# Transposing attention probabilities in 32x32 blocks on VectorE with SBUF-to-SBUF transfers, and a new order of the first loads

## The chip, the cores and the metric

The kernel runs on one core of a Trainium2 chip. The metric is the time of one execution on the device in microseconds (us), and lower is better.

## What is computed

One encoder layer runs over two token sequences, a prompt of 512 tokens and a sample of 1024, laid side by side as 1536 tokens of width 1024, all in float32:

```python
h = RMSNorm(x)
a_val, a_glu, z_a, q, k, v, z_b, g_logits = split(h @ w_in)         # 9 x 1024 columns
y_a = (silu(LayerNorm(conv31(a_val * sigmoid(a_glu)))) * silu(z_a)) @ w_pw_a
# 16 heads; every query sees an 8 x 16 window of the (rows, 64) token grid, with a learned bias
p = softmax(where(valid, q @ k.T / 8 + bias, -1e30))
y_b = ((p @ v) * silu(z_b)) @ w_o_b
x + (sigmoid(g_a) * y_a + sigmoid(g_b) * y_b) @ w_out               # then a final RMSNorm
```

## The kernel before, in words

**Matrix products.** Every float32 operand is kept as a high and a low part, and a product of 128x128 weights with 512 tokens is three matmuls (low x high, high x low, high x high). A group is one 128-column tile of the weights times 512 tokens: 8 contraction steps, 24 matmuls into one of two PSUM banks (pg). Half a group, 12 matmuls, is called a slot, and slots are the clock by which all engines' instruction lists are written.

**Prologue.** SP loads the token tiles x and the first weight pieces (L409 to L424). ACT's queue issues six loads of small parameters and the load of norm_g (L655 to L658). VectorE multiplies each token tile by its reciprocal norm and norm_g (`normalise`, L1011), TensorE transposes it (`h_t`), ACT writes the high part and VectorE the low part (`h_hi`, `h_lo`). Then v is projected, and the tiles of the first head pair.

**Units.** There are 8 units, one for each pair of heads. Unit 0 and unit 7 are written out and have 36 slots each, units 1 to 6 are a hardware loop body of 48 slots. In each unit TensorE projects the next tiles while attention of the head pair is woven in between. Attention has 12 blocks of 128 queries in each unit. A block sees 256 keys (blocks 0 to 3) or 384 keys (blocks 4 to 11), for each of two heads. Blocks are taken in pairs. `pair_at` puts a pair at slot 1 and then every `2 * spacing(i)` slots: 4 slots in units 0 and 7, 6 slots in the loop. The work of a pair goes like this:

- At its slot TensorE first does `values` of the pair before (L1464, which waits for pt_ok), and then `scores` (L1435) into four PSUM banks pS.
- VectorE adds bias and mask and takes the minimum (`scores`, L1143), ACT takes the exponential with its sum (L841), VectorE takes the reciprocal (L1151) and multiplies (L1153). The first block of the pair is done in the pair's slot, the second one slot later, behind a convolution tap (`tap`, L1069) and the evacuation of a group.
- `transposed_at` sets the slots at which TensorE transposes the probabilities 128x128 at a time into PSUM (`transposes`, L1455, 512 of them), and ACT copies them back to SBUF (`probs_t`, L844).
- `take_o` (L1155) multiplies the result in PSUM bank pO by the gate.

**SP's queue.** SP runs down one list. In a unit it loads weight pieces (`piece`, L394), each behind a wait for the low part of the piece that held the buffer (w_lo), then the relative bias of the next unit (`load_rel`, 16 transfers) and its v (`load_v`, 16 transfers, behind pv_done). Behind unit 7 it waits for pv_done of all blocks and loads seven tiles of 768 KB of the gated attention (tb_d, L497), which ACT and VectorE split in `refill_tb` (L765), called at slots 33 and 35 of unit 7 and behind it.

GpSimd builds the bias tiles (L580) as VectorE frees them.

Of the kernel before, what the change touches and what calls it, by code (L numbers as in the profile page):

```python
# [24 lines left out]
F32 = mybir.dt.float32  # L25
# [79 lines left out]
def spacing(i):  # L105

    return 2 if isinstance(i, int) else 3
# [40 lines left out]
def build(nc, x_prompt, x_sample, norm_g, w_in, b_gate, dw_w, dw_b, ln_g, ln_b, w_pw_a, rpb,  # L148
          w_o_b, w_out, final_g, masks, y_prompt, y_sample):
    with ExitStack() as ctx:  # L150
# [26 lines left out]
        tt = take(4 * 384).rearrange("p (s n) -> p s n", s=4)  # L177
        pt = take(4 * 384).rearrange("p (s n) -> p s n", s=4)
# [75 lines left out]
        pT = ctx.enter_context(nc.psum_tensor("pT", [P, CH], F32))  # L254
        pO = ctx.enter_context(nc.psum_tensor("pO", [P, CH], F32))

        pH = [pT, pO, pS[2], pS[3]]
# [34 lines left out]
        tr_done, pt_ok, pv_done, o_out = (sem(n) for n in ("tr_done", "pt_ok", "pv_done", "o_out"))  # L292
# [82 lines left out]
        def transposed_at(i, slot, half):  # L375

            m = 4 * spacing(i)
            c, r = divmod(2 * slot + half - 2, m)
            t = r - (6 if spacing(i) == 3 else 4)
            if 0 <= t < 4 and 0 <= c < BLOCKS // 2:  # L380
                return 2 * c + t // 2, t % 2
            return None
# [10 lines left out]
        def _(sp):  # L393
# [16 lines left out]
            for s in range(4):  # L410
                piece_s(s, w_rows(w0, C_V * P, s))
                if s % 2:
                    load_x(1 + s // 2)
            for t in range(3, 8):
                load_x(t)
            for s in range(4, 6):
                piece_s(s, w_rows(w0, C_V * P + CH, s - 4))

            sp.wait_ge(w_lo, 4)
            sp.dma_start(msk32, masks).then_inc(mask_in, 16)  # L420
            for t in range(8, NT):
                load_x(t)
# [35 lines left out]

            def unit(i):
# [5 lines left out]
                for n, c in enumerate(ahead):  # L465
                    s = s_of(i) + n + 2
                    piece(s, w_tile(w0, i * P + c * P), 8 * i + (s - 1))
                    if n == len(ahead) - 3 and not last:
                        load_rel(i + 1, 18 * i + 18)
                    if n == len(ahead) - 2 and not last:  # L470
                        load_v(i + 1, BLOCKS * i + BLOCKS)
# [6 lines left out]
            def piece_y(s):  # L478
                if s < S_OUT:
                    piece_s(s, w_tile(w_o_b[0] if s < S_YA else w_pw_a[0], (s - S_YB) % KT * P))  # L480
                else:
                    piece_s(s, w_rows(w_out[0], CH * ((s - S_OUT) // 4), (s - S_OUT) % 4))

# [5 lines left out]

            piece_y(S_YB)  # L490
            piece_y(S_YB + 1)
# [55 lines left out]
        def _(pool):  # L547
# [21 lines left out]
            def unit(i):  # L569
                for kd in range(KINDS):  # L570
                    for h in range(2):
                        s, jk = kd // 3, kd % 3
                        nk = SEG_ROWS[s] * BAND
                        if kd == 0:
# [6 lines left out]
                            bt[:, 2 * (kd % 2) + h, 0:nk].rearrange("p (r c) -> p r c", c=BAND),  # L581
                            mask[:, KIND_OFF[kd]:KIND_OFF[kd] + nk].rearrange("p (r c) -> p r c", c=BAND),
                            e, ALU.subtract).then_inc(bias_ok, 1)
# [41 lines left out]
        def _(act):  # L625
# [29 lines left out]
            for r, n, src in ((0, TAPS, dw_w[0]), (I_DWB, 1, dw_b[0:1, :]), (I_LNG, 1, ln_g[0:1, :]),  # L655
                              (I_LNB, 1, ln_b[0:1, :]), (I_BGA, 1, b_gate[0:1, 0:D]), (I_BGB, 1, b_gate[0:1, D:2 * D])):
                act.dma_start(prow[r:r + n, :], src).then_inc(par_in, 16)
            act.dma_start(ngb, norm_g[0:1, :].to_broadcast([P, D])).then_inc(ng_in, 16)  # L658

# [8 lines left out]
            def h_hi(t):  # L668
                for hf in range(2):
                    act.wait_ge(ht_ps, 2 * t + hf + 1)  # L670
                    nc.scalar.activation(xs[:, 4 * hf:4 * hf + 4, 0, t * P:(t + 1) * P],
                                         pH[(2 * t + hf) % 4][:].rearrange("p (k n) -> p k n", k=4),
                                         ACT.Copy).then_inc(x_hi, 1)
# [15 lines left out]
            split_s(0)  # L689
            split_s(1)  # L690
            square(1)
            h_hi(0)
            split_s(2)
            split_s(3)
            for t in range(NT):
                if t + 2 < NT:
                    square(t + 2)
                if t + 1 < NT:
                    h_hi(t + 1)
                    take_v(t)  # L700
                if t == 4:
                    split_s(4)
# [68 lines left out]
            def unit(i):  # L771
# [64 lines left out]
                def probs(b, h):  # L836
# [3 lines left out]
                    t = tt[:, x, 0:keys_of(b)]  # L840
# [3 lines left out]
                def probs_t(b, h):  # L844
                    act.wait_ge(tr_done, blk(i, b, h))

                    after(act, pv_done, BLOCKS * i + max(b - 1, 0))
                    nk = keys_of(b)
                    nc.scalar.activation(pt[:, buf(b, h), 0:nk], pT[:, 0:nk], ACT.Copy).then_inc(pt_ok, 1)  # L849

                for slot in range(2 * NCH * len(tiles)):
# [9 lines left out]
                    for half in range(2):  # L861
                        bh = transposed_at(i, slot, half)
                        if bh is not None:
                            probs_t(*bh)
# [12 lines left out]
                    if slot == spacing(i) * BLOCKS + 2 and not last:  # L877
# [105 lines left out]
        def _(dve):  # L983
# [29 lines left out]
            def h_lo(t):  # L1013
                for hf in range(2):
                    dve.wait_ge(x_hi, 2 * t + hf + 1)
                    nc.vector.tensor_tensor(xs[:, 4 * hf:4 * hf + 4, 1, t * P:(t + 1) * P],
                                            pH[(2 * t + hf) % 4][:].rearrange("p (k n) -> p k n", k=4),
                                            xs[:, 4 * hf:4 * hf + 4, 0, t * P:(t + 1) * P].bitcast(F32),
                                            ALU.subtract).then_inc(x_lo, 1)

            mean_square_x(0)
            split_s(0)
            normalise(0)
            split_s(1)
            mean_square_x(1)
            h_lo(0)
            split_s(2)
            normalise(1)
            split_s(3)
            for t in range(1, NT):  # L1030
                if t + 1 < NT:
                    mean_square_x(t + 1)
                h_lo(t)
                if t + 1 < NT:
                    normalise(t + 1)
                if t == 5:
                    split_s(4)
                    dve.wait_ge(par_ps, 1)
                    nc.vector.tensor_copy(par[:].rearrange("p k n -> p (k n)"), pS[0][:, 0:KT * NPAR]).then_inc(par_ok, 1)
# [7 lines left out]
            for s in range(5, 10):  # L1047
                split_s(s)
# [81 lines left out]
            def unit(i):  # L1130
# [4 lines left out]
                def scores(b, h):  # L1135
# [4 lines left out]
                    after(dve, tr_done, 24 * i + max(blk(0, b - 2, h), 0))  # L1140
# [3 lines left out]
                        out=tt[:, x, 0:nk], in0=pS[x][:, 0:nk], in1=bt[:, 2 * (kind_of(b) % 2) + h, 0:nk], scale=1.0,  # L1144
                        scalar=3e38, op0=ALU.add, op1=ALU.min, accum_out=mn[:, x:x + 1]).then_inc(t_ok, 1)

                def probs(b, h):
                    x = buf(b, h)
                    t = tt[:, x, 0:keys_of(b)]
# [3 lines left out]
                    nc.vector.tensor_scalar(t, t, rinv[:, x:x + 1], None, ALU.mult).then_inc(p_ok, 1)  # L1153

                def take_o(s):  # L1155
# [6 lines left out]
                    o = pO[:].rearrange("p (j r c) -> p j r c", j=4, c=QB)  # L1162
# [22 lines left out]
                for slot in range(slots):  # L1185
# [5 lines left out]
                    if c is not None and c >= 2 and c % 2 == 0:  # L1191
                        take_o(c // 2 - 1)
                    if c is not None and c < BLOCKS // 2:
# [3 lines left out]
                        for h in range(2):  # L1197
                            probs(2 * c, h)
                    c = late_pair_at(i, slot)
# [150 lines left out]
        def _(pe):  # L1350
            PASSES = ((1, 0), (0, 1), (0, 0))

            def half_group(b, s, n, hf, ready=None, midway=None):
# [227 lines left out]
```

## Time and profile before

| | |
|---|---|
| median of 3 runs | 1835.28 us (1830.8 to 1837.01) |
| the profiled execution | 1836.65 us, its span 1834.8 us |
| TensorE matmul busy | 1795.8 us, 98% of the span |
| VectorE, ScalarE, GpSimd busy | 1093.2, 549.8, 210.0 us |
| mean granted TensorE clock | 0.994 |
| DMA on SP's queue | 111.44 MB, 20.3% of 16 engines' span |

The profile is of one execution. Busy time of an engine is the time in which one of its instructions ran. Matmuls are pipelined, so what one costs is read from the distance between starts, not from its own duration. SPq and ACTq are the instructions by which a queue issues transfers, and they are not counted as busy time.

### The profile page before, as it was taken

How to read it: one execution, taken by the hardware profiler on the slowest of the kernel's cores; microseconds unless marked ns; L12 is line 12 of the kernel's file. 1: busy time of each engine (PE TensorE's matmuls, PEld its weight loads, DVE VectorE, ACT ScalarE, POOL GpSimd, SP SyncE). 2: the span in 40 equal slices, each digit the busy share in tenths (PEclk: the TensorE clock that was granted, in tenths of full speed). 3: DMA queues.
4: the chain of work that ended last, by engine and by line, in shares of the span. 5: the costliest groups of instructions: out<-in, count | busy, mean ns of one | idle time of the engine just before them, and what ended most of it. 6: DMA issues, size and time to landing. Idle time of an engine off the chain costs nothing.

```text
span 1834.8 us, 25369 instructions
## 1 busy us (share of the span) xinstructions
PE 1795.8 (98%) x9164; PEld 1463.8 (80%) x9164; DVE 1093.2 (60%) x1573; ACT 549.8 (30%) x1117; POOL 210.0 (11%) x250
## 2 busy tenths in 40 slices
PE   6999999999999999999999999999999999999998
PEld 5888878888888888888888888888887777888786
DVE  3410695785587387558648837856874667535432
ACT  4411134233223323313322332332345233202122
POOL 0030011011011101101101110110110045000001
PEclk9999999999999999999999999999999999999999
DMA  7163101312211221231230223123116756543223
GB/s 272 53 116 92 41 30 53 92 58 87 75 42 64 78 73 52 81 88 47 86 87 30 69 70 87 53 81 87 35 58 240 253 156 200 167 137 104 92 81 126
DMA packets 163357, 174.03 MB, mean 95 GB/s; under 512 B 11238, under 2 KB 117750, under 8 KB 163098
## 3 DMA queue, kind: packets, MB, share of 16 engines
q1 hardware_dynamic: 136848, 111.44, 20.3%
q10 hardware_dynamic: 22506, 47.08, 6.8%
q0 software_dynamic: 3872, 13.75, 3.0%
q8 instruction: 84, 1.38, 0.3%
q14 instruction: 47, 0.39, 0.1%
HBM read 121.55 MB, written 50.68 MB: 94 GB/s over the span
## 4 chain that ended last, share of the span: by engine, by line
PE 89%; DVE 5%; DMA 3%; ACT 1%; issue 1%; SPq 0%; ACTq 0%; POOLq 0%; POOL 0%; DVEq 0%
PE pg L1361 65%; PE pg L1379 14%; PE pO L1476 3%; PE pT L1461 3%; PE pS L1451 3%; DVE work L1255 1%; DMA qk<-gb_d 1%; DVE work L1069 1%; DMA work<-tb_d 1%; DMA work<-in_norm_g 1%; DVE ws L987 1%; DVE xs L995 0%; ACT xs L763 0%; ACT ws L631 0%; DVE work L1261 0%
## 5 line engine op out<-in xcount | busy, mean ns | idle before, releaser
L1361 PE MATMUL pg<-xs,ws 128*128 128x512 f32 x5760 | 1384.1, 396 | 7.0 <-DVE work L1272 7.0
L1361 PEld LDWEIGHTS pg<-xs,ws 128*128 128x128 f32 x5760 | 1068.2, 189 | 233.8 <-issue 14.8
L1069 DVE SCALAR_TENSOR_TENSOR work<-work 128x1551 f32<-128x1551 f32 x240 | 449.4, 1873 | 4.1
L1379 PE MATMUL pg<-ws,xs 128*128 128x512 f32 x1008 | 239.8, 394 | 3.0 <-DVE ws L987 2.4
L1379 PEld LDWEIGHTS pg<-ws,xs 128*128 128x128 f32 x1008 | 189.8, 190 | 44.5 <-DVE ws L987 3.7
L987 DVE TENSOR_TENSOR ws<-raw,ws 128x1024 fp32r<-128x1024 f32 x90 | 109.9, 1222 | 137.3 <-ACT ws L631 137.2
L1143 DVE CUSTOM_DVE_ANT_0 work<-pS,work 128x384 f32<-128x384 f32 (+1 forms) x192 | 88.8, 511 | 166.1 <-PE pS L1451 165.7
L580 POOL TENSOR_TENSOR work<-work 128x384 f32<-128x384 bf16 (+1 forms) x72 | 63.1, 877 | 1052.3 <-DVE small L1143 1039.2
L841 ACT ACTIVATE work<-work,small 128x384 f32<-128x384 f32 (+1 forms) x192 | 109.2, 570 | 218.3 <-DVE small L1143 218.3
L849 ACT ACTIVATE work<-pT 128x384 f32<-128x384 f32 (+1 forms) x192 | 87.3, 454 | 170.3 <-PE pT L1461 170.2
L631 ACT ACTIVATE ws<-raw 128x1024 fp32r<-128x1024 f32 x90 | 94.6, 1053 | 110.3 <-PE pg L1361 83.3
L1153 DVE TENSOR_SCALAR work<-work,small 128x384 f32<-128x384 f32 (+1 forms) x192 | 97.5, 508 | 6.8
L1461 PEld LDWEIGHTS pT<-ident,work 128*128 128x128 f32 x512 | 67.7, 140 | 26.8 <-DVE work L1153 1.7
L1461 PE MATMUL pT<-ident,work 128*128 128x128 f32 x512 | 87.0, 272 | 1.3 <-DVE work L1153 1.3
L580 POOL TENSOR_TENSOR work<-work,ws 128x384 f32<-128x384 bf16 (+1 forms) x72 | 66.5, 924 | 55.2 <-DMA ws<-rel_d 55.2
L1476 PEld LDWEIGHTS pO<-work 128*64 128x64 f32 x1024 | 54.9, 137 | 17.0 <-issue 17.0
L1476 PE MATMUL pO<-work 128*64 128x128 f32 x1024 | 66.5, 277 | 0.0
L1095 DVE SCALAR_TENSOR_TENSOR work<-work 128x512 f32<-128x512 f32 x24 | 17.6, 731 | 75.4 <-ACT work L813 62.9
L1328 DVE TENSOR_TENSOR work<-pg,work 128x512 f32<-128x512 f32 x24 | 16.6, 692 | 75.3 <-PE pg L1379 75.2
L1276 DVE SCALAR_TENSOR_TENSOR work<-qk,pg 128x512 f32<-128x512 f32 x24 | 16.5, 687 | 73.2 <-PE pg L1361 73.2
L824 ACT ACTIVATE work<-pg,work 128x512 f32<-128x512 f32 x48 | 33.0, 687 | 74.1 <-PE pg L1361 74.0
L1163 DVE TENSOR_TENSOR work<-pO,work 128x512 f32<-128x512 f32 x24 | 16.6, 691 | 57.5 <-PE pO L1476 57.5
(100 smaller groups left out, 960.8 us busy)
## 6 DMA issues: line engine op xcount, KB each, us to landing
raw<-in_w_in SPq DMA_DIRECT2D x70, 512.0 KB, 3.8
work<-v_d SPq DMA_DIRECT2D x128, 96.0 KB, 3.0
v_d<-work ACTq DMA_DIRECT2D x24, 256.0 KB, 2.0
za_d<-work ACTq DMA_DIRECT2D x24, 256.0 KB, 2.0
ga_d<-work ACTq DMA_DIRECT2D x24, 256.0 KB, 2.0
gb_d<-work ACTq DMA_DIRECT2D x24, 256.0 KB, 2.0
work<-c_d POOLq DMA_DIRECT2D x8, 768.0 KB, 13.2
qk<-gb_d SPq DMA_DIRECT2D x24, 256.0 KB, 4.0
```

Of the source, the lines that this page charges most:

```text
L580: nc.gpsimd.tensor_tensor(bt[:, 2 * (kd % 2) + h, 0:nk].rearrange("p (r c) -> p r c", c=BAND), mask[:, KIND_OFF[kd]:KIND_OFF[kd] + nk].rea ...
L631: nc.scalar.activation(wt(s, 0), raw_of(s), ACT.Copy).then_inc(w_hi, 1)
L841: nc.scalar.activation(t, t, ACT.Exp, scale=-1.0, bias=mn[:, x:x + 1], accum_out=rsum[:, x:x + 1]).then_inc(p_exp, 1)
L849: nc.scalar.activation(pt[:, buf(b, h), 0:nk], pT[:, 0:nk], ACT.Copy).then_inc(pt_ok, 1)
L987: nc.vector.tensor_tensor(wt(s, 1), raw_of(s), wt(s, 0).bitcast(F32), ALU.subtract).then_inc(w_lo, 1)
L1069: nc.vector.scalar_tensor_tensor(cv[:, 0:CLEN], u[:, k:k + CLEN], cur[:, k:k + 1], cv[:, 0:CLEN], ALU.mult, ALU.add).then_inc(tap_ok, 1)
L1143: nc.vector.tensor_tensor_reduce(out=tt[:, x, 0:nk], in0=pS[x][:, 0:nk], in1=bt[:, 2 * (kind_of(b) % 2) + h, 0:nk], scale=1.0, scalar=3e38 ...
L1153: nc.vector.tensor_scalar(t, t, rinv[:, x:x + 1], None, ALU.mult).then_inc(p_ok, 1)
L1361: last = nc.tensor.matmul(pg[b][:], wt(s, wpart)[:, k * P:(k + 1) * P], xs[:, k, xpart, chunk(n)], start=(k == 0 and wpart == 1), stop=(k ...
L1379: last = nc.tensor.matmul(pg[b][:], xs[:, k, xpart, t * P:(t + 1) * P], wt(s0 + k // 2, wpart)[:, chunk(k % 2)], start=(k == 0 and xpart = ...
L1461: mm = nc.tensor.transpose(pT[:, c * P:(c + 1) * P], tt[:, buf(b, h), c * P:(c + 1) * P], ident[:])
L1476: mm = nc.tensor.matmul(pO[rows, j * P:(j + 1) * P], vb[:, SEG_RG[s] + c, j, rows], pt[:, buf(b, h), c * P:(c + 1) * P], start=(c == 0), s ...
```

## The change

The 128x128 transposes on TensorE and ACT's copies go. VectorE transposes each head's probabilities in place, as a grid of 32x32 blocks, right behind the multiplication. SP then moves the blocks between partition groups: for each block of queries 16 transfers (4 source groups of 32 partitions times 4 target groups), of 32 partitions x 2 heads x 256 or 384 bytes each. The keys are ordered by quadrant so that each quarter is contiguous; scores, bias, mask and values follow that order. A semaphore for each block parity (p_in) lets `values` start. pT's PSUM bank becomes a second bank of pO, and `take_o` comes behind scores and the first probabilities. A pair comes every 5 slots in units 0 and 7 and every 6 in the loop, as `pair_at` divides by `spacing(i)` now. SP's `move_probs` of a pair stands behind the weight piece of the same index. In the last unit the pieces S_YB and S_YB+1 move in between. In the prologue norm_g and the small parameters are loaded by SP, norm_g second; x tiles come later than the first weight pieces; `params` on TensorE comes behind the first 12 token groups, and `normalise(0)` ahead of the first split on VectorE.

```diff
 def spacing(i):
-    return 2 if isinstance(i, int) else 3
+    return 5 if isinstance(i, int) else 6
...
         def pair_at(i, slot):
-            c, r = divmod(slot - 1, 2 * spacing(i))
+            c, r = divmod(slot - 1, spacing(i))
...
             load_x(0)
-            for s in range(4):
+            sp.dma_start(ngb, norm_g[0:1, :].to_broadcast([P, D])).then_inc(ng_in, 16)
+            for s in range(2):
                 piece_s(s, w_rows(w0, C_V * P, s))
-                if s % 2:
-                    load_x(1 + s // 2)
-            for t in range(3, 8):
+            load_x(1)
+            for s in range(2, 4):
+                piece_s(s, w_rows(w0, C_V * P, s))
+            for t in range(2, 8):
                 load_x(t)
...
+            def move_probs(i, b):
+                nk, n = keys_of(b), b % 2
+                x = nk // 4
+                sp.wait_ge(tr_done, blk(i, b, 1))
+                for a in range(4):
+                    for g in range(4):
+                        src = tt[32 * a:32 * a + 32, n, 0:2 * nk].rearrange("p (h n) -> p h n", h=2)[:, :, g * x:g * x + x]
+                        dst = pt[32 * g:32 * g + 32, n, 0:2 * nk].rearrange("p (h n) -> p h n", h=2)[:, :, a * x:a * x + x]
+                        sp.dma_start(dst, src).then_inc(p_in[n], 16)
...
+                for n in range(8):
+                    if n < len(ahead):
+                        s = s_of(i) + n + 2
+                        piece(s, w_tile(w0, i * P + ahead[n] * P), 8 * i + (s - 1))
+                    elif last and n < 6:
+                        piece_y(S_YB + n - 4)
+                    if n < BLOCKS // 2:
+                        move_probs(i, 2 * n)
+                        move_probs(i, 2 * n + 1)
+                    if n == 4 and not last:
+                        load_rel(i + 1, 18 * i + 18)
+                    if n == len(ahead) - 2 and n >= 6 or n == 5 and len(ahead) == 6:
+                        load_v(i + 1, BLOCKS * i + BLOCKS)
...
                     nc.vector.tensor_scalar(t, t, rinv[:, x:x + 1], None, ALU.mult).then_inc(p_ok, 1)
+                    dve.wait_ge(p_ok, blk(i, b, h))
+                    nc.vector.transpose(t, t).then_inc(tr_done, 1)
...
-                def transposes(b, h):
-                    pe.wait_ge(p_ok, blk(i, b, h))
-                    after(pe, pt_ok, blk(i, b, h) - 1)
-                    for c in range(keys_of(b) // P):
-                        mm = nc.tensor.transpose(pT[:, c * P:(c + 1) * P], tt[:, buf(b, h), c * P:(c + 1) * P], ident[:])
-                    mm.then_inc(tr_done, 1)
...
                 def values(b):
-                    pe.wait_ge(pt_ok, blk(i, b, 1))
+                    pe.wait_ge(p_in[b % 2], 1536 * i + 256 * (b // 2) + 256)
```

## Rows read from the trace of the kernel before

**Rows 1.** The page's first part: TensorE's busy time and share.
```profile
PE 1795.8 (98%) x9164; PEld 1463.8 (80%) x9164; DVE 1093.2 (60%) x1573; ACT 549.8 (30%) x1117; POOL 210.0 (11%) x250
```

**Rows 2.** The chain that ended last, share of the span by line.
```profile
PE pg L1361 65%; PE pg L1379 14%; PE pO L1476 3%; PE pT L1461 3%; PE pS L1451 3%; DVE work L1255 1%; DMA qk<-gb_d 1%; DVE work L1069 1%; DMA work<-tb_d 1%; DMA work<-in_norm_g 1%; DVE ws L987 1%; DVE xs L995 0%; ACT xs L763 0%; ACT ws L631 
```

**Rows 3.** Costliest groups: TensorE's transposes of the probabilities.
```profile
L1461 PE MATMUL pT<-ident,work 128*128 128x128 f32 x512 | 87.0, 272 | 1.3 <-DVE work L1153 1.3
```

**Rows 4.** Timeline of TensorE in the loop: start us, duration us, instructions.
```profile
781.07 0.49 PE L1461 MATMUL pT<-ident,work 128*128 128x128 f32 x3
...
782.79 0.49 PE L1461 MATMUL pT<-ident,work 128*128 128x128 f32 x3
...
790.76 1.53 PE L1476 MATMUL pO<-work 128*64 128x128 f32 x24
792.22 33.06 PE L1361 MATMUL pg<-xs,ws 128*128 128x512 f32 x144
...
843.68 1.09 PE L1476 MATMUL pO<-work 128*64 128x128 f32 x16
844.70 0.39 PE L1451 MATMUL pS<-qk,ws 64*128 64x256 f32 x2
```

**Rows 5.** Timeline of all engines around two pairs of blocks in the loop.
```profile
845.61 8.47 PE L1361 MATMUL pg<-xs,ws 128*128 128x512 f32 x36
...
848.09 0.83 DVE L1153 TENSOR_SCALAR work<-work,small 128x256 f32<-128x256 f32 x1
...
864.22 0.45 PE L1451 MATMUL pS<-qk,ws 64*128 64x384 f32 x2
...
865.28 0.56 DVE L1143 CUSTOM_DVE_ANT_0 work<-pS,work 128x384 f32<-128x384 f32 x1 [0.17 <-PE pS L1451]
...
865.49 4.80 PE L1361 MATMUL pg<-xs,ws 128*128 128x512 f32 x20
...
867.20 0.16 DVE L1151 RECIPROCAL small<-small 128x1 f32<-128x1 f32 x1
...
868.07 0.42 DVE L1153 TENSOR_SCALAR work<-work,small 128x384 f32<-128x384 f32 x1
```

**Rows 6.** Timeline of SP's queue: runs of transfers, in unit 0 and the loop.
```profile
124.84 3.61 SPq L432 DMA_DIRECT2D work<-rel_d  x8
...
169.49 8.60 SPq L441 DMA_DIRECT2D work<-v_d  x16
...
608.46 3.79 SPq L432 DMA_DIRECT2D ws<-rel_d  x8
...
763.18 3.79 SPq L432 DMA_DIRECT2D ws<-rel_d  x8
```

**Rows 7.** Time from issue to landing of the transfers of line 432.
```profile
DMA to landing us min/median/max: 1.8/2.0/3.4
```

**Rows 8.** TensorE behind a stop, then a window: us, busy by engine, PEclk, DMA.
```profile
235.77 0.39 PE L1451 MATMUL pS<-qk,ws 64*128 64x256 f32 x2 [2.20 <-DVE ws L1109]
...
236.79 7.18 PE L1361 MATMUL pg<-xs,ws 128*128 128x512 f32 x24
...
252.27 5.75 PE L1361 MATMUL pg<-xs,ws 128*128 128x512 f32 x24
...
236.50:239.90 3.40, 3.40 (x12) 2.54 (x10) 3.33 (x3) 0.00 (x0) 0.00 (x0) 0.50 0.02 5
```

**Rows 9.** Timeline of SP and ScalarE in unit 7, and line 497's landing.
```profile
1385.47 3.43 SPq L497 DMA_DIRECT2D work<-tb_d  x7
...
DMA to landing us min/median/max: 5.4/10.3/15.1
...
1403.59 4.28 ACT L763 ACTIVATE xs<-work 128x512 fp32r<-128x512 f32 x8 [0.23 <-DMA work<-tb_d]
```

**Rows 10.** Timeline of the prologue.
```profile
8.14 0.55 POOL L556 TENSOR_TENSOR small<-small 128x1 f32<-128x1 f32 x1 [6.63 <-DVE small L1002]
...
16.20 1.28 DVE L1011 SCALAR_TENSOR_TENSOR work<-work,small 128x1024 f32<-128x1024 f32 x1 [2.12 <-DMA work<-in_norm_g]
```

More of the change, by code:

```diff
@@ L291, in build @@
             sem(n) for n in ("qk_hi", "qk_done", "t_ok", "p_exp", "inv_ok", "p_ok"))
-        tr_done, pt_ok, pv_done, o_out = (sem(n) for n in ("tr_done", "pt_ok", "pv_done", "o_out"))
+        tr_done, pv_done, o_out = (sem(n) for n in ("tr_done", "pv_done", "o_out"))
+        p_in = [sem(f"p_in{n}") for n in range(2)]
         tbs_in, c_in = sem("tbs_in"), [sem(f"c_in{k}") for k in range(KT)]
@@ L373, in late_pair_at, with head_of, by_quadrant @@
             return pair_at(i, slot - 1) if slot >= 2 else None
[L375 to L382, printed above, removed]
+        def head_of(a, b, h):
+            return a[:, b % 2, h * keys_of(b):(h + 1) * keys_of(b)]
+        def by_quadrant(ap, w):
+            return ap.rearrange("p (c g w) -> p g c w", g=4, w=w)
         def after(eng, sm, count):
@@ L666, in square, with h_hi @@
                                      accum_out=ssq[:, t:t + 1]).then_inc(sq_ok, 1)
[L668 to L673, printed above, removed]
+            def h_hi(t, hf):
+                act.wait_ge(ht_ps, 2 * t + hf + 1)
+                nc.scalar.activation(xs[:, 4 * hf:4 * hf + 4, 0, t * P:(t + 1) * P],
+                                     pH[(2 * t + hf) % 4][:].rearrange("p (k n) -> p k n", k=4),
+                                     ACT.Copy).then_inc(x_hi, 1)
             def take_v(g):
@@ L698, in _ @@
                 if t + 1 < NT:
-                    h_hi(t + 1)
+                    for hf in range(2):
+                        h_hi(t + 1, hf)
                     take_v(t)
@@ L876, in unit @@
                         act.dma_start(row_of(c_d, i)[:, PROMPT:TOK], cv[:, PROMPT + PAD:CLEN]).then_inc(c_out, 16)
-                    if slot == spacing(i) * BLOCKS + 2 and not last:
+                    if slot == spacing(i) * (BLOCKS // 2) + 2 and not last:
                         act.wait_ge(o_out, NCH * i + NCH)
@@ L1011, in normalise, with h_lo @@
                 nc.vector.scalar_tensor_tensor(x, x, rstd[:, t:t + 1], ngb, ALU.mult, ALU.mult).then_inc(xn_ok, 1)
[L1013 to L1019, printed above, removed]
+            def h_lo(t, hf):
+                dve.wait_ge(x_hi, 2 * t + hf + 1)
+                nc.vector.tensor_tensor(xs[:, 4 * hf:4 * hf + 4, 1, t * P:(t + 1) * P],
+                                        pH[(2 * t + hf) % 4][:].rearrange("p (k n) -> p k n", k=4),
+                                        xs[:, 4 * hf:4 * hf + 4, 0, t * P:(t + 1) * P].bitcast(F32),
+                                        ALU.subtract).then_inc(x_lo, 1)
             mean_square_x(0)
+            normalise(0)
             split_s(0)
-            normalise(0)
+            h_lo(0, 0)
             split_s(1)
+            h_lo(0, 1)
             mean_square_x(1)
-            h_lo(0)
+            normalise(1)
             split_s(2)
-            normalise(1)
             split_s(3)
@@ L1032, in _ @@
                     mean_square_x(t + 1)
-                h_lo(t)
+                for hf in range(2):
+                    h_lo(t, hf)
                 if t + 1 < NT:
@@ L1046, in _ @@
             nc.vector.memset(u[:, ULEN - PAD:ULEN], 0.0).then_inc(pads_ok, 1)
-            for s in range(5, 10):
+            for s in range(5, 8):
+                split_s(s)
+            dve.wait_ge(par_ps, 1)
+            nc.vector.tensor_copy(par[:].rearrange("p k n -> p (k n)"), pS[0][:, 0:KT * NPAR]).then_inc(par_ok, 1)
+            for s in range(8, 10):
                 split_s(s)
@@ L1198, in unit @@
                             probs(2 * c, h)
+                    if c is not None and c >= 2 and c % 2 == 0:
+                        take_o(c // 2 - 1)
                     c = late_pair_at(i, slot)
@@ L1351, in _, with half_group @@
             PASSES = ((1, 0), (0, 1), (0, 0))
-            def half_group(b, s, n, hf, ready=None, midway=None):
+            def half_group(b, s, n, hf, ready=None):
                 for k in range(4 * hf, 4 * hf + 4):
-                    if k % 4 == 2 and midway is not None:
-                        midway()
                     if ready is not None:
@@ L1470, in values @@
                     if j == 0:
-                        after(pe, o_out, NCH * i + s)
+                        after(pe, o_out, NCH * i + (1 if s == 2 else 0))
                     for c in range(nc_):
@@ L1490, in unit @@
                         scores(2 * c + 1)
-                    bh, midway = transposed_at(i, slot, 0), None
-                    if bh is not None:
-                        transposes(*bh)
-                    bh = transposed_at(i, slot, 1)
-                    if bh is not None:
-                        midway = functools.partial(transposes, *bh)
                     if hf == 0:
```

89 lines of the change are left out of this document (35 added, 54 removed).

## The prediction

> **What bounds the kernel now.** I read the page first: TensorE is busy 98% of the span [rows 1]. The chain that ended last says the same by line: products 65% and 14%, and values, transposes and scores 3% each [rows 2]. So a TensorE instruction that goes is worth its whole pitch, provided that nothing makes TensorE wait. The page's groups give 512 transposes with only 1.3 us of idle time before them [rows 3]: the attention chain keeps up today.
>
> The timeline of TensorE gives the pitches [rows 4]. 144 product matmuls take 33.06 us, 0.2295 us each, so a slot of 12 takes 2.755 us. From one group of three transposes to the next are 1.72 us; six matmuls take 1.38 of it, and three transposes 0.345. Values of a pair take 1.46 us (384 keys) or 1.02 (256 keys). Scores of a pair take 845.61 - 844.70 = 0.9 us or 865.49 - 864.22 = 1.28 us [rows 4, 5]. These add up to a loop unit: 48 slots 132.2, values 2 x 1.02 + 4 x 1.46 = 7.9, scores 2 x 0.9 + 4 x 1.28 = 6.9, 64 transposes 7.4, in all 154.4 us. Measured between the same transfers of two passes: 763.18 - 608.46 = 154.7 [rows 6]. By the same terms unit 0 or unit 7 has 36 slots, 99.2 + 7.9 + 6.9 + 7.4 = 121.4 us.
>
> **The gain.** 512 transposes at 0.115 us are 59 us of TensorE. ACT's 192 copies also go, but ACT is not in the chain; they count nothing.
>
> **The new chain of a pair.** Let T be the start of the first product behind a pair's scores, 865.49 in [rows 5]. VectorE begins the scores at 865.28, the first reciprocal at 867.20, and ends the second multiplication at 868.49, T + 3.0. Two transposes stand in this stretch now, each behind a wait for the multiplication. No row shows one. The nearest are 0.42 us (the multiplication of the same 384 columns) and 0.83 us (256 columns while GpSimd works) [rows 5]; I take 0.5 and 0.1 for the wait, as these are SBUF to SBUF at 384 columns. So the first block is transposed at T + 4.2; with the bounds T + 4.0 to T + 4.9.
>
> Then SP issues 16 transfers for the first block and 16 for the second. The second block's transposes come behind a tap (1.8 us), an evacuation (0.7) and two more multiplications and transposes (2.4), at about T + 9.5, when SP is still at the first 16. So SP is the limit, and what counts is the pitch of an issue. Eight issues with constant addresses took 3.61 us, 0.45 each; sixteen took 8.60, 0.54 each; eight in the loop with address arithmetic took 3.79, 0.47 each [rows 6]. Each is a small transfer as here (16 to 32 partitions, 48 to 96 KB against 16 to 24 KB), and none comes below 0.45. I take 0.47, with 0.45 and 0.54 as ends. The 32nd issue starts 31 x 0.47 = 14.6 us behind the first. From there to landing are 2.0 us, ends 1.8 and 3.4 [rows 7], and 0.1 until TensorE goes on. The second block is there at 4.2 + 14.6 + 2.0 + 0.1 = T + 20.9.
>
> **Where TensorE stands then.** In the loop it reaches `values` after 6 slots, T + 16.5, does the first block (there since T + 13.4) and waits from T + 17.2 for 3.7 us. In units 0 and 7 there are 5 slots, T + 13.8, and the wait is 6.4 us. Behind it stand the second block's values (0.5 or 0.75 us) and the next scores, so the period of a pair is set by this chain, whatever the spacing.
>
> Per unit: 6 x 20.9 = 125.4, values of the odd blocks 2 x 0.5 + 4 x 0.75 = 4.0, scores 6.9: 136.3 us. Outside the pairs lie 12 slots in the loop (33.1 us) and 6 in units 0 and 7 (16.5). That gives 169.4 and 152.8 us against 154.7 and 121.4. The loss is 6 x 14.7 = 88 us in the loop and 2 x 31.4 = 63 us in the other two. The gain of the transposes is inside these figures.
>
> **The clock.** After a stop of 2.20 us the granted clock was 0.50, the 1.2 GHz level, for 3.4 us, and 24 matmuls took 7.18 us in place of 5.75 [rows 8]. Each of the 48 pairs now has a longer stop. Where the slow stretch falls on products it is hidden, as TensorE waits anyway. Where it falls on the 2 us of values and scores behind the stop, it doubles them. Between 0 and 2.0 us a pair, 0 to 96 us in all; I take 0.5, as the drop in [rows 8] began 0.7 us behind the stop and left the scores nearly untouched: 24 us.
>
> **What else moves.** (1) In unit 7 the last values come at slot 31, not 25, and SP loads seven tiles only behind them. The seven loads took 3.4 us of issues and up to 15.1 to land, 18.1 us from the first issue to ScalarE's start [rows 9]. Today this is hidden; now only 5 slots, 13.8 us, are left. Products of the next phase need the first parts 1.3 us later, at 19.4, and the second group after them waits for two refills of 4.28 us and two evacuations of 0.7 on ScalarE, 28.5 us against 19.3: 9 us lost. (2) In the prologue the reciprocal norm was ready at 8.7 us and `normalise` started at 16.20, waiting for norm_g [rows 10]. At most 7.5 us can be won, at least nothing, as the same bytes come in; I take 6, since norm_g stands second and VectorE's split behind `normalise`. (3) Waits on SP: a weight piece now stands behind 32 moves, some 20 us later than its buffer is free, but it is split 12 slots (33 us) after. `load_rel` costs 16 x 0.5 = 8 us on SP behind the fifth pair, and ends about when the sixth pair's transposes do: nothing, or 1 us a unit. `load_v` comes as now. (4) Moved `take_o` has a second bank as cover. VectorE gains 192 x 0.6 = 115 us in a longer span; it stays far from full.
>
> **Sum.** 1836.65 (the profiled execution, 0.1% over the median of 1835.28) + 88 + 63 + 24 + 9 - 6 = 2015 us, 10% slower.
>
> The Trainium skill, DMA: Bandwidth & Descriptors, Rules for kernel authors, warns against many small transfers, since under 64 KB mostly overhead is paid, and its section Anatomy of one DMA puts that fixed part at about 2.0 us. If the 32 fixed parts came one behind another, a pair would take over 60 us and the kernel some 2000 us more. [Rows 6, 7] speak against that reading: eight transfers of 2.0 us each were issued within 3.8 us, so they overlap, and only the issue pitch adds up.
>
> **The rivals.**
>
> *Issues are cheap enough, and the kernel gets faster.* The place is SP between the first block's transposes and TensorE's `values`. With transfers issued every 0.32 us the second block is there at 4.2 + 9.9 + 2.1 = T + 16.2, ahead of T + 17.2 in the loop. In units 0 and 7 12 pairs wait 1.8 us each, 21 us. Time: 1836.65 - 59 + 21 + 9 - 6 = 1802 us. It decides at a pitch of 0.35. For it speaks only that these transfers are smaller; against it all four runs of issues in [rows 6]. Chance 8%. The Trainium skill, DMA: Bandwidth & Descriptors, Issuing engines are not separate DMA queues, says that the sequencer's time to start a transfer is usually small beside the transfer. By that rule this rival would hold, and the trace disagrees: 0.45 to 0.54 us of issue against 2.0 us of transfer, times 32.
>
> *Each move costs more than loads from HBM do.* Short pieces of 256 and 384 bytes between partition groups, 2048 pairs of reads and writes for a pair of blocks, beside weight loads on the same engines. At 0.6 us a move the period grows by 31 x 0.13 = 4.0 us, 48 pairs 193 us: 2208 us. The 0.54 of the sixteen loads, one of them held up, points there [rows 6]. Chance 12%.
>
> *No measurable change*, the waits just cancelling the gain: 1%. About 0.3% is what a measurement of this kernel can tell from no change.
>
> The forecast has 79%. Its own bounds: pitch 0.45 to 0.54 is -30 to +104 us, landing -10 to +67, transposes -10 to +34, the clock -24 to +72; not all at one end, so about 1940 to 2110. That range holds 8 in 10 with a small part of the third case; I keep it. Faster 9%, the same 1%, slower 90%.
>
> **What would show it.** In the profile after: no transposes of pT; idle time of TensorE before L1476's successor of some 3 to 4 us in the loop and 6 in units 0 and 7, released by DMA pt<-tt; SP's queue showing 32 issues over about 15 us for each pair; a loop unit of about 169 us; PEclk with many slices below full; VectorE's transposes at 0.4 to 0.8 us. I am wrong if the issue pitch is under 0.4 us, if the landing is far from 2 us, or if TensorE waits for VectorE and not for DMA.

## The result and the profile after

The changed kernel takes 2319.74 us (median of 4 runs, 2318.96 to 2320.43) against 1836.14 us, a ratio of 1.2639 with a 95% interval of 1.2624 to 1.2654. The direction was the forecast one. The size was not: 484 us were lost where 180 were expected, and the time lies outside the range of 1940 to 2110.

The page of the changed kernel, parts 1, 2 and 4:

```profile
span 2318.5 us, 25531 instructions
PE 1850.3 (80%) x8652; PEld 1494.4 (64%) x8652; DVE 1177.1 (51%) x1765; ACT 467.9 (20%) x925; POOL 209.8 (9%) x250
...
PEclk9999778888988898889889888988897789999999
...
SPq 40%; PE 37%; DVE 11%; issue 6%; DMA 5%; ACT 1%; DVEq 1%; POOLq 0%; POOL 0%; ACTq 0%
SPq L477 39%; PE pg L1366 20%; PE pg L1384 11%; DMA work<-work 4%; PE pO L1472 3%; PE pS L1455 3%; DVE work L1158 2%; DVE work L1160 2%; DVE work L1148 1%; DVE work L1262 1%; DVE work L1074 1%; DMA work<-tb_d 1%; DMA qk<-gb_d 0%; DVE small 
```

TensorE was busy 98% of the span [rows 1] and is busy 80% now. In the chain that ended last the products had 65% and 14% [rows 2]; now SP's issues on line 477, the moves, have 39%. The PEclk row has the digits 7 and 8 in most slices of the stretch of the units, where the kernel before had 9 throughout.

The waits of TensorE in the changed kernel (us in all, times, longest):

```profile
PE pO L1472 <- DMA work<-work: 428.7, 63, 9.8
PE pg L1366 <- DVE work L1279: 8.1, 4, 6.8
PE pO L1400 <- DVE work L1013: 7.7, 1, 7.7
PE pg L1366 <- ACT work L837: 7.3, 1, 7.3
```

The first of these is `values`, which waits 428.7 us for the moves. That is the place that the prediction named, but its size is about twice the forecast one (36 x 3.7 + 12 x 6.4 = 210 us). One pair in the loop, in the timelines of SP's queue and of TensorE:

```profile
913.13 21.27 SPq L477 DMA_DIRECT2D work<-work  x32
...
943.92 20.72 SPq L477 DMA_DIRECT2D work<-work  x32
```

```profile
909.27 16.90 PE L1366 MATMUL pg<-xs,ws 128*128 128x512 f32 x72
926.10 0.88 PE L1472 MATMUL pO<-work 128*64 128x128 f32 x12
935.69 1.55 PE L1472 MATMUL pO<-work 128*64 128x128 f32 x12 [8.71 <-DMA work<-work]
937.17 0.69 PE L1455 MATMUL pS<-qk,ws 64*128 64x384 f32 x2
...
939.38 6.96 PE L1366 MATMUL pg<-xs,ws 128*128 128x512 f32 x27
```

32 moves are issued in 21.27 us, 0.66 us each, where [rows 6] show 0.45 to 0.54 for loads. (The pitch of an issue, below, is the distance from the start of one to the start of the next.) TensorE does its six slots and the first block's values, stops for 8.7 us, and then does the second block's values and the scores in 3.69 us (939.38 - 935.69), where full rate gives 2.0.

The instructions of line 477, then the two moves by size with their time to landing:

```profile
L477 SPq DMA_DIRECT2D work<-work x1536: 585/597/1702, 234.3 to 1867.8; - x192
...
work<-work SPq DMA_DIRECT2D x1024, 24.0 KB, 1.9
...
work<-work SPq DMA_DIRECT2D x512, 16.0 KB, 1.8
```

An issue takes 597 ns (the median; 585 is the least, 1702 the most), and the next starts 42 ns behind it: a pitch of 0.639 us, the same for 256 and 384 keys. Four of the sixteen moves of a block stay in their own group of 32 partitions, and they too have medians of 594 to 597 ns, so it is not the way from group to group that is paid for.

A pair's period, cut in the traces at the starts of instructions (means over the 40 pairs that scores follow):

| part | predicted, us | after, us | e8, us | e12, us |
|---|---|---|---|---|
| first product to first move | 4.2 | 3.97 | 4.01 | 4.15 |
| first to last issue | 14.6 | 20.40 | 15.16 | 20.72 |
| last issue to second block's values | 2.1 | 1.87 | 1.87 | 1.87 |
| values and scores to the next first product | 2.35 (0.5 of it the clock) | 3.37 | 2.95 | 2.11 |
| sum | 23.2 | 29.6 | 24.0 | 28.8 |

### The profile page after: what moved, and what is told of

The parts are those of the page before. It is cut to its first block, busy times and chain, and to the rows that moved or that the text cites. A ratio compares the mean times of both kernels' runs of the same rounds, so it can differ in the third digit from the quotient of the medians.

```text
span 2318.5 us, 25531 instructions
## 1 busy us (share of the span) xinstructions
PE 1850.3 (80%) x8652; PEld 1494.4 (64%) x8652; DVE 1177.1 (51%) x1765; ACT 467.9 (20%) x925; POOL 209.8 (9%) x250
## 4 chain that ended last, share of the span: by engine, by line
SPq 40%; PE 37%; DVE 11%; issue 6%; DMA 5%; ACT 1%; DVEq 1%; POOLq 0%; POOL 0%; ACTq 0%
SPq L477 39%; PE pg L1366 20%; PE pg L1384 11%; DMA work<-work 4%; PE pO L1472 3%; PE pS L1455 3%; DVE work L1158 2%; DVE work L1160 2%; DVE work L1148 1%; DVE work L1262 1%; DVE work L1074 1%; DMA work<-tb_d 1%; DMA qk<-gb_d 0%; DVE small L1148 0%; DVE xs L997 0%
## 5 line engine op out<-in xcount | busy, mean ns | idle before, releaser
L1366 PEld LDWEIGHTS pg<-xs,ws 128*128 128x128 f32 x5760 | 1111.5, 194 | 276.9 <-issue 32.7
L1472 PE MATMUL pO<-work 128*64 128x128 f32 x1024 | 106.0, 356 | 428.7 <-DMA work<-work 428.7
L1074 DVE SCALAR_TENSOR_TENSOR work<-work 128x1551 f32<-128x1551 f32 x240 | 440.2, 1834 | 4.1
L1472 PEld LDWEIGHTS pO<-work 128*64 128x64 f32 x1024 | 75.2, 178 | 458.3 <-DMA work<-work 446.3
L1160 DVE STREAM_TRANSPOSE work<-work 128x384 f32<-128x384 f32 (+1 forms) x192 | 102.6, 534 | 6.6
L737 ACT ACTIVATE qk<-pg 128x512 fp32r<-128x512 f32 x24 | 14.3, 598 | 196.6 <-PE pg L1366 175.6
L1455 PE MATMUL pS<-qk,ws 64*128 64x384 f32 (+1 forms) x192 | 52.0, 539 | 2.2 <-DVE ws L1114 2.2
L997 DVE SCALAR_TENSOR_TENSOR xs<-work,xs 128x512 fp32r<-128x512 f32 x72 | 44.1, 684 | 13.6 <-ACT xs L776 13.6
```

The lines of the kernel that those rows point to most:

```text
L1074: nc.vector.scalar_tensor_tensor(cv[:, 0:CLEN], u[:, k:k + CLEN], cur[:, k:k + 1], cv[:, 0:CLEN], ALU.mult, ALU.add).then_inc(tap_ok, 1)
L1160: nc.vector.transpose(t, t).then_inc(tr_done, 1)
L1366: last = nc.tensor.matmul(pg[b][:], wt(s, wpart)[:, k * P:(k + 1) * P], xs[:, k, xpart, chunk(n)], start=(k == 0 and wpart == 1), stop=(k ...
L1455: mm = nc.tensor.matmul(pS[buf(b, h)][:, 0:nk].rearrange("p (g c w) -> p g c w", g=4, w=BAND), q, k, start=qpart is q_lo, stop=kpart is k_ ...
L1472: mm = nc.tensor.matmul(pO[s % 2][rows, j * P:(j + 1) * P].rearrange("p (a q) -> p a q", a=4), vb[:, SEG_RG[s] + c, j, rows], p[:, c], sta ...
```

## The experiments

All of them keep the rest of the changed kernel, if nothing else is said. e1, e2, e3, e5, e6 and e8 are one run each. Code is shortened, with `...` where something is left out. T is the start of the first product behind a pair's scores, as in the prediction. Theory A: the period is the time that one queue needs to issue 32 moves in a row, and one issue costs 0.64 us because of where its two ends lie. Rivals: B, an issue costs by its many short pieces, and C, the data engines push back.

**e1, half the pieces and bytes.** The moves of head 1 are left out, so its product reads old probabilities.

```diff
-src = tt[...].rearrange("p (h n) -> p h n", h=2)[:, :, g * x:g * x + x]
+src = tt[...].rearrange("p (h n) -> p h n", h=2)[:, 0:1, g * x:g * x + x]
```
and the same for dst.

> The moves carry head 0 only, so each transfer has 32 pieces in place of 64; head 1's product uses stale probabilities (this part of the result is left out). Theory A (an issue costs 0.64 us because the source lies in SBUF, whatever it carries): pitch still 0.64 us, time within 1% of the changed kernel's 2320 us. Theory B (an issue costs by its short pieces): pitch nearer to 0.45 to 0.55, each 0.1 us less is worth 31 x 0.1 x 48 = 150 us, so 2030 to 2170 us. Theory C (the data engines push back): like B, as half the bytes and pieces move.

2298.12 us, 22 less than the changed kernel. Its issues, instructions of line 477:

```profile
L477 SPq DMA_DIRECT2D work<-work x1536: 507/591/1798, 234.4 to 1846.1; - x192
```

591 ns in place of 597. Halving bytes and pieces leaves the price of an issue as it is, so B and C fall for this pattern. (The 22 us come from a run of issues that is 0.35 us shorter in each pair, 17 us, and from small parts of the rest.)

**e2 and e3, one end in HBM.** The same 16 transfers of the same pieces, read from a scratch tensor in HBM that one store fills (e2), or written to it and brought back by one load (e3).

```diff
+sp.dma_start(p_d[n, :, 0:2 * nk], tt[:, n, 0:2 * nk]).then_inc(d_in[n], 16)
+sp.wait_ge(d_in[n], 96 * i + 16 * (b // 2) + 16)
-        src = tt[32 * a:32 * a + 32, n, 0:2 * nk]...
+        src = p_d[n, 32 * a:32 * a + 32, 0:2 * nk]...
```

> One store of the transposed block to a scratch tensor in HBM, a wait, and then the same 16 transfers per block with the same pieces, but read from HBM. Theory A: pitch of the 16 falls to the 0.45 to 0.48 us of the weight and bias loads; each block pays about 2.6 us for store and wait, so the second block is there at 4 + 2 x 2.6 + 32 x 0.47 + 1.9 = T + 26 and the time is about that of the changed kernel, 2280 to 2340 us. Theories B and C: pitch stays 0.64, T + 31.5, about 2570 us.

> The same 16 transfers per block with SBUF as source write to HBM, then one load of 128 partitions brings the block back. If the source side in SBUF sets the pitch: 0.64 us stays and the time rises by about 5 us a pair, 2550 us. If only the combination of SBUF on both sides costs 0.64, the pitch falls to 0.45 to 0.5 and the time is about 2300 us. If the pieces set it: 0.64 or more.

2474.43 and 2457.28 us. No expected time fits. The timeline of SP's queue in e2, a block with 256 keys and a block with 384:

```profile
923.73 7.35 SPq L481 DMA_DIRECT2D work<-p_d  x16
```

```profile
304.74 10.10 SPq L481 DMA_DIRECT2D work<-p_d  x16
```

With 256 keys a transfer has a pitch of 0.470 us, with 384 keys 0.637, in both kernels. Within one kernel the same line has two prices. What differs is that with 384 keys a row of the scratch tensor (768 elements) is exactly two heads long, so partition and head can fold into one dimension on the HBM side. The trace of e3 has it so: the target of such a transfer is one dimension of 64 pieces, where with 256 keys it is 2 x 32.

**e5 and e6, the fold taken away.**

```diff
-p_d = scratch("p_d", [2, P, 768])
+p_d = scratch("p_d", [2, P, 800])
```

> As e2, with rows of 800 instead of 768 elements in the scratch tensor. In e2 the pitch was 0.47 us in blocks with 256 keys and 0.637 in blocks with 384, where a row is exactly two heads long, so that on the HBM side the partition and head dimensions fold into one of 64 and the two sides no longer have the same shape. Theory A2 (same shapes on both sides and one side in HBM: 0.47; SBUF on both sides or unlike shapes: 0.64): now 0.47 in all blocks, and the time falls by about 32 pairs x 31 x 0.167 = 166 us, to about 2310 us. If the length of the piece (384 bytes) costs instead, the 0.637 stays and the time stays near 2474 us.

> As e3 with rows of 800 elements. Theory A2: SBUF as source alone does not cost, pitch 0.47 in all blocks, time about 2457 - 166 = 2290 us. If the source in SBUF costs for 384-byte pieces, 0.637 stays and so does the time.

2301.24 and 2279.77 us, 173 and 178 us less by 32 elements of padding, and both within 11 us of what was expected. In the trace of e6 the target is 2 x 32 pieces in all blocks. The instructions of the 16 transfers in e5 and then in e6:

```profile
L481 SPq DMA_DIRECT2D work<-p_d x1536: 302/427/1837, 237.0 to 1849.5; - x192
```

```profile
L479 SPq DMA_DIRECT2D p_d<-work x1536: 302/427/1984, 234.8 to 1826.3; - x192
```

427 ns with SBUF as target alone and with SBUF as source alone, 597 with SBUF at both ends, for the same pieces. With the 42 to 43 ns between issues that is a pitch of 0.470 us, the one that the prediction took. So neither the short piece nor SBUF as a source costs, but both ends in SBUF, or two ends of unlike shape. Why the queue needs longer for these is open; no run here shows it.

**e4, through HBM with five transfers a block.** One store, a wait, and a load for each target group.

```diff
+sp.dma_start(p_d[n].rearrange("h p m -> p h m")[:, :, 0:nk],
+             tt[:, n, 0:2 * nk].rearrange("p (h m) -> p h m", h=2)).then_inc(d_in[n], 16)
+sp.wait_ge(d_in[n], 96 * i + 16 * (b // 2) + 16)
+for g in range(4):
+    src = p_d[n].rearrange("h (a p) m -> p (h a) m", a=4)[:, :, g * x:g * x + x]
+    dst = pt[32 * g:32 * g + 32, n, 0:2 * nk].rearrange("p (k q) -> p k q", k=8)
+    sp.dma_start(dst, src).then_inc(p_in[n], 16)
```

> One store of the transposed block to HBM and four loads (one for each target group of 32 partitions, 256 pieces each) in place of 16 moves. If the number of issues on SP is what the changed kernel pays for, the second block is there at about T + 9.5 + 2.6 + 4 x 0.47 + 2 = T + 16, ahead of T + 17.2 in the loop and 1.5 us late in units 0 and 7: 1836 - 59 (transposes) - 10 (first loads) + 8 (end of unit 7) + 18 = about 1793 us, and the granted clock is back at 0.99. If short pieces cost by themselves (theory B or C: 1024 pieces a block as before), the four loads take as long as the 16 moves did, 10 us a block, and the time stays above 2150 us.

1817.54 us, ratio to the kernel before 0.9899 (0.9874 to 0.9923): 502 us under the changed kernel and 1% under the kernel before, with the same 1024 pieces of 256 or 384 bytes a block. Its loads of 256 pieces each have a pitch of 0.49 us, so it is the number of issues that is paid for and not that of pieces. SP's queue and TensorE in the timeline of e4:

```profile
893.06 0.38 SPq L475 DMA_DIRECT2D p_d<-work  x1
895.87 1.80 SPq L481 DMA_DIRECT2D work<-p_d  x4
897.78 0.39 SPq L475 DMA_DIRECT2D p_d<-work  x1
900.51 1.78 SPq L481 DMA_DIRECT2D work<-p_d  x4
```

```profile
888.77 16.61 PE L1370 MATMUL pg<-xs,ws 128*128 128x512 f32 x72
905.31 1.53 PE L1476 MATMUL pO<-work 128*64 128x128 f32 x24
```

The second block's last issue ends 13.5 us behind the first product (902.3 - 888.8) and the values of both blocks run in one piece. TensorE's waits are 22.7 us for the loads, 8.0 for ScalarE behind unit 7 and 5.2 for VectorE in unit 0:

```profile
PE pO L1476 <- DMA work<-p_d: 22.7, 20, 3.4
PE pg L1370 <- ACT work L841: 8.0, 1, 8.0
...
PE pg L1370 <- DVE work L1188: 5.2, 2, 3.0
```

The time is 24 us above the expected 1793, 7 of it in the loop and some 18 in units 0 and 7. From scores to scores a loop pass takes 148.6 us (154.8 before). Unit 0 takes 139.2 us against 125.1 before, and unit 7, up to the first product behind it, 137.2 against 122.3: in these two the granted clock is 0.95 and 0.94 (0.99 and 1.00 before), 17.3 of the 22.7 us of waits for the loads fall there, and so do the other two waits.

**e7, the issues shared by two queues.** SP issues source groups 0 and 1, ScalarE's queue 2 and 3, one and three slots behind the pair's slot.

```diff
-for a in range(4):
+for a in (0, 1):                     # SP
...
+for late in range(2):                # ScalarE's list, in every slot
+    c = pair_at(i, slot - 1 - 2 * late) if slot >= 2 + 2 * late else None
+    if c is not None and c < BLOCKS // 2:
+        move_probs(2 * c + late)     # for a in (2, 3)
```

> Half of the moves (source groups 2 and 3) are issued by ScalarE's queue, one slot and three slots after the pair's slot; SP issues the other half. Theory A (what counts is the time that one sequencer needs for each issue, 0.64 us x 32 in a row): each queue issues 16, the second block is there at about T + 16.5, no wait in the loop and 2 us in units 0 and 7: 1800 to 1860 us, somewhat more if ScalarE's late evacuations hold up TensorE. If both queues share one generator or the data engines are the limit, the 32 still take 20 us: about 2300 us.

1916.13 us, ratio 1.0436 (1.0358 to 1.0514), 404 us faster than the changed kernel with the same 1536 moves. So it is the issue on one sequencer that counts, and two queues issue side by side: in the timelines of SP and ScalarE's queue

```profile
1017.01 10.59 SPq L477 DMA_DIRECT2D work<-work  x16
```

```profile
1017.02 5.43 ACTq L866 DMA_DIRECT2D work<-work  x8
```

both have 0.66 to 0.68 us a move at the same time. It misses the expected 1860 for two reasons. TensorE's waits show the first, 52.5 us for the moves where 12 pairs with 2 us each were expected:

```profile
PE pO L1487 <- DMA work<-work: 52.5, 26, 4.3
PE pg L1381 <- DVE work L1199: 18.4, 9, 2.2
PE pg L1381 <- ACT work L837: 11.7, 2, 9.7
PE pg L1381 <- DVE work L1195: 11.5, 6, 1.9
```

The second is that issues on ScalarE's list hold up its other work. The timelines of ScalarE, VectorE and TensorE in one place of the loop:

```profile
372.86 5.42 ACTq L866 DMA_DIRECT2D work<-work  x8
378.47 1.06 ACT L648 ACTIVATE ws<-raw 128x1024 fp32r<-128x1024 f32 x1 [5.40 <-PE pg L1381]
```

```profile
379.56 1.23 DVE L1004 TENSOR_TENSOR ws<-raw,ws 128x1024 fp32r<-128x1024 f32 x1 [2.57 <-ACT ws L648]
...
384.32 0.68 DVE L1195 SCALAR_TENSOR_TENSOR work<-work,pg 128x512 f32<-128x512 f32 x1
```

```profile
385.15 3.01 PE L1381 MATMUL pg<-xs,ws 128*128 128x512 f32 x12 [1.91 <-DVE work L1195]
```

The high part of a weight piece stands behind eight issues, VectorE waits 2.57 us for it, and its evacuation of a group, which stands behind that and two convolution taps, ends so late that TensorE waits 1.91 us for the bank.

**e8, 12 of 16 moves.**

```diff
-for g in range(4):
+for g in range(3):
```
with the counts of p_in to match. The last target group is left out, so a quarter of the probabilities is old.

> Only 12 of the 16 moves of a block (the last target group is left out, so a quarter of the probabilities is stale). The chain of a pair is 8 x 0.64 = 5.1 us shorter: the second block is there at about T + 20.8, which is the T + 20.9 of the prediction. If the issues in a row set the period, the time is 2320 - 48 x 5.1 = 2075 us. What it lies above the prediction's 2015 us is then what the prediction's other terms (the clock above all) missed. If the time hardly falls, something else than the issues sets the period.

2058.13 us, 262 us less for 8 issues fewer a pair: 5.5 us for each of the 48 pairs. Eight pitches are 5.1, and the last part of the period is 0.42 shorter, as stops of 3.9 us in place of 8.6 leave less of the slow clock. Here the run of issues takes 15.16 us, about what the prediction assumed, and the time is 43 us over the predicted 2015. The run of issues gives 27 us of that (0.56 in 48 pairs) and the last part of the period 24 (2.95 against 2.35 in 40 pairs); an earlier first move and a faster landing give some 15 back, and the rest is not traced.

**e9, the first loads alone.** The kernel before with only the prologue of the change.

> The kernel before with only the new order of the first loads. The first scores came 10.1 us earlier in the changed kernel (225.65 against 235.77 us). If that part stands by itself: 1836 - 10 = 1826 us, ratio 0.9945. If it was given back or lost later: no difference.

1824.5 us, ratio 0.9947 (0.9933 to 0.9961). The part stands by itself. Against it the rest of the change cost 495 us.

**e10, part of unit 7's loads ahead of the last values** (on top of e4).

```diff
-sp.wait_ge(pv_done, BLOCKS * PAIRS)
+sp.wait_ge(t_ok, BLK * PAIRS)
+sp.wait_ge(bias_ok, 18 * PAIRS)
 sp.wait_ge(tap_ok, TAPS * PAIRS)
-for k in range(7):
+for k in (2, 4, 5, 6):
+    sp.dma_start(home(k), tb_d[k]).then_inc(tbs_in, 16)
+sp.wait_ge(pv_done, BLOCKS * PAIRS)
+for k in (0, 1, 3):
     sp.dma_start(home(k), tb_d[k]).then_inc(tbs_in, 16)
```

> As e4 (through HBM, 5 transfers a block), and behind unit 7 four of the seven tiles of gated attention, whose place is free before the last values, are loaded before the wait for them. If the 8 us for which TensorE waited for ScalarE at the start of the next phase come from these late loads, most of it goes: 1817.5 - 6 = 1811 us. If something else held ScalarE, the time stays at 1817.

1816.48 us, ratio 0.9903 (0.9886 to 0.9919), which is not distinct from e4. TensorE's wait for ScalarE went from 8.0 to 6.1 us in the profile. From the first load behind the last values to ScalarE's first refill 18.4 us pass in e4 (1370.57 to 1388.99); with three loads there in place of seven they are still 15.0 (1368.67 to 1383.62). A miss.

**e11 and e12, TensorE kept busy in the stop.**

```diff
 values(2 * c - 2)
+after(pe, t_ok, 24 * i + 4 * c)
+for _ in range(60):                  # 32 in e12
+    nc.tensor.matmul(pS[3][:, 0:P], ident[:], ident[:], start=True, stop=True)
 values(2 * c - 1)
```

> The changed kernel with 60 matmuls of the identity (into a free PSUM bank, results unused, about 7.3 us) between the values of a pair's first and second block, where TensorE waits for the moves anyway. If the stop lowers the clock and the slow clock then stretches the second block's values and the scores (3.7 us in place of 2.0), that goes, as the moves land at the same time: 48 x 1.6 = 77 us less, about 2245 us. If the clock costs nothing in this chain, the time stays at 2320; it rises if the extra work comes out later than the moves.

> As e11, with 32 extra products in place of 60. In e11 each took two instructions of 0.114 us, 13.7 us a pair, 5 us more than the stop they were to fill, so its time says nothing of the clock; its rows show values and scores behind them at full rate (2.07 us from the second block's first matmul to the next product, against 3.69 in the changed kernel). 32 take 7.3 us and fit into the stops of 7.2 to 9.8 us. If the slow clock behind the stop is part of a pair's chain: 2320 - 48 x 1.6 = about 2245 us. If it costs nothing: 2320 us.

e11: 2476.9 us, as the extra products took 13.7 us a pair. No stop is left in it, and values and scores take 1.92 us in the mean. e12: 2300.65 us, ratio 1.2555 (1.2531 to 1.258), 19 us less than the changed kernel, not 75. The table above tells why. Values and scores take 2.11 us in place of 3.37, so at least 1.26 us of a pair's period was the slow clock. But the run of issues is 0.32 us longer and the first move comes 0.18 later in the mean, and 2.4 us later in the sixth pair of a unit (6.5 against 4.1 us, medians), where SP is now still issuing `load_rel`. One pair of e12 in TensorE's timeline:

```profile
971.92 0.88 PE L1472 MATMUL pO<-work 128*64 128x128 f32 x12
972.73 7.41 PE L1485 MATMUL pS<-ident 128*128 128x128 f32 x64
981.61 0.88 PE L1472 MATMUL pO<-work 128*64 128x128 f32 x12 [1.46 <-DMA work<-work]
982.41 0.44 PE L1455 MATMUL pS<-qk,ws 64*128 64x384 f32 x2
...
983.68 1.65 PE L1366 MATMUL pg<-xs,ws 128*128 128x512 f32 x6
```

Behind a stop of 1.46 us the second block's values and the scores take 2.07 us, full rate. The granted clock of the run is 0.976 (0.891 in the changed kernel).

## Why the prediction was wrong

**The mechanism was right.** TensorE waits in `values` for the moves, SP's issues in a row set the period, the spacing of pairs does not matter (a period has 29.6 us in the loop with its 6 slots and in units 0 and 7 with their 5), and VectorE is not in the way: the first move came 3.97 us behind the first product, against 4.2 predicted, and a transpose of 384 columns took 0.578 us against 0.5. Landing came out at 1.8 to 1.9 us against 2.0. At the second block TensorE waited for the moves in all 48 pairs. e7 and e8 confirm that the number of issues on one queue is what is paid for.

**The step that failed** is the pitch of an issue, "I take 0.47, with 0.45 and 0.54 as ends". It measured 0.639 us in the middle, and 0.66 with the held-up ones (20.40 us over 31 steps). That lies beyond the upper end, which itself came from sixteen loads of which one was held up; without it the loads of [rows 6] have pitches of 0.46 to 0.50 us in the trace. The rows it was taken from were all loads from HBM; none had SBUF at both ends, and e5 and e6 show that exactly this difference is worth 0.17 us. The sum, its bounds and the list of signs (which looked for a pitch under 0.4, not for a larger one) all took rows of another kind as if they bounded this kind. Even with every term at its upper end the prediction gives 2015 + 104 + 67 + 34 + 72 = 2292 us, less than the measured 2320. The difference, 5.8 us a pair times 48, is 278 us of the 305 that were missing; the last part of the period, with the clock in it, is 41 (3.37 against 2.35 in 40 pairs), and the other terms nearly cancel.

**The clock** was a term of 24 us and cost more. Values and scores take 3.37 us in place of the 1.92 of e11, 1.45 us in each of the 40 pairs that scores follow. The second block's values alone take 1.48 in place of 0.81 in the other eight. That is 63 us in all, inside the bounds of 0 to 96. The reason for taking only 0.5 a pair was that behind a stop of 2.20 us the clock fell 0.7 us after it [rows 8]. Here the stops have 8.6 us in the mean, and the clock falls inside them: in the pair above the stop ends at 935.69, and the granted clock is 0.50, the 1.2 GHz level, from 930.4 to 940.6. It covers values and scores whole. Two windows, the stop with values and scores, and the products before it (us, busy by engine, PEclk, DMA):

```profile
926.00:939.40 13.40, 4.69 (x38) 3.58 (x37) 0.80 (x4) 0.07 (x1) 0.03 (x1) 0.66 0.26 67
910.00:926.00 16.00, 16.00 (x72) 13.02 (x70) 15.61 (x23) 4.83 (x11) 1.16 (x2) 1.00 0.26 76
```

**The first loads** gave 10.1 us in the profile (first scores at 225.65 against 235.77 us) and 11 in the runs of e9, more than the 7.5 that was called the most. The bound took the reciprocal norm's 8.7 us [rows 10] as fixed, but the first x tile and weight piece also came in earlier: ScalarE starts on them at 4.08 and 7.76 us, before it was 6.72 and 11.76. The prologue in the changed kernel:

```profile
4.08 1.06 ACT L677 ACTIVATE work<-work 128x1024 f32<-128x1024 f32 x1 [2.05 <-DMA work<-in_x_prompt]
...
6.29 1.29 DVE L1013 SCALAR_TENSOR_TENSOR work<-work,small 128x1024 f32<-128x1024 f32 x1 [0.88 <-DMA work<-in_norm_g]
```

`normalise` starts at 6.29 us in place of 16.20.

**The end of unit 7**: 9 us expected. TensorE waits 7.3 us for ScalarE there and 6.8 us for VectorE two groups on, 14.0 in all. The kernel before had two waits in this stretch, 3.8 us together, so about 10 were lost. In the kernel before:

```profile
1423.83 16.61 PE L1361 MATMUL pg<-xs,ws 128*128 128x512 f32 x72 [0.97 <-DVE work L1272]
1443.31 29.09 PE L1361 MATMUL pg<-xs,ws 128*128 128x512 f32 x120 [2.86 <-DVE work L1272]
```

**The rivals.** The second one, a price of 0.6 us a move and 2208 us, was the nearest, and its chance of 12% too low. Its reason was wrong: half the pieces cost the same (e1), and the same pieces from HBM cost 0.47 (e5). That its price was near is luck. The first, that issues are cheap, is refuted for 32 moves but shows what the idea was worth: with 10 issues a pair (e4) the transposes off TensorE do pay in the loop. Of the 59 us, 44 lie there; a pass in e4 takes 148.2 us (906.65 - 758.45 between the same loads) against 154.7, 39 us in six passes. Most of that is lost again in units 0 and 7 and behind: 11 of the 18 us by which e4 beats the kernel before are the first loads (e9), so the new way of transposing is worth 7 us (1817.54 against 1824.5). The fixed part of about 2.0 us that the prediction takes from the Trainium skill (DMA: Bandwidth & Descriptors, Anatomy of one DMA) is stated there for transfers that GpSimd issues. SP's moves landed in 1.8 to 1.9 us here, so the argument built on it stands.

## What to carry to other kernels

Count the transfers between two waits and multiply by the issue pitch of their own kind: for small transfers in a row this, and not bytes or landing time, is the length of the chain. A bound taken from rows of another kind (here HBM loads for moves within SBUF) is not a bound; the range must be wider by that. Where a layout change needs 16 transfers within SBUF, one store to HBM and four loads back were 500 us faster here. Against the kernel before with only its first loads reordered that gained 7 us, as the shorter units still had to wait.

## What the runs showed of the hardware

- An issue on SP's queue took 0.427 us with one end in HBM (e5, e6) and 0.597 with both in SBUF, for the same 64 pieces of 256 or 384 bytes; 32 pieces took 0.591 (e1).
- With one end in HBM, 0.427 became 0.594 (e2) and 0.595 (e3) where a row pitch of 768 elements let two dimensions fold on that side only, and went back to 0.427 with 800 (e5, e6).
- SP's and ScalarE's queues issued side by side at 0.66 to 0.68 us each (e7), as SP alone did (0.66).
- Landing of a 16 or 24 KB move within SBUF took 1.8 to 1.9 us from the start of its issue, where the loads in [rows 7] had 2.0.
- In a stop of TensorE from 926.98 to 935.69 us the granted clock fell to 0.50 at 930.4 and came back at 940.6, 4.9 us after work had begun again; behind a stop of 1.46 us in e12 values and scores ran at full rate.
